# A signal for each bank of a product in a two-block transformer kernel, and gate logits inside the value product

## What is computed

```python
def hybrid_mixer(h, w_in, b_f, conv_w, conv_b, conv_ln_g, conv_ln_b, w_o):
    proj = h @ w_in
    q, k, v, f_logit, conv_val, conv_gate = jnp.split(proj, splits, axis=-1)
    log_f = jax.nn.log_sigmoid((f_logit + b_f).astype(jnp.float32))
    attn = fox_attention(q, k, v, log_f)          # causal, + cumsum(log_f)[t] - cumsum(log_f)[s]
    u = conv_val * jax.nn.sigmoid(conv_gate)
    u = causal_depthwise_conv(u, conv_w, conv_b)  # 31 taps
    u = jax.nn.silu(layer_norm_2(u, conv_ln_g, conv_ln_b))
    return jnp.concatenate([attn, u], axis=-1) @ w_o

def swiglu_ffn(h, w_ffn_in, w_ffn_out):
    g, u = jnp.split(h @ w_ffn_in, 2, axis=-1)
    return (jax.nn.silu(g) * u) @ w_ffn_out
```

## Time and profile before

| | |
|---|---|
| median of 3 runs | 2511.76 us (2510.68 to 2514.68) |
| span of the profiled execution | 2521.1 us |
| mean granted clock of TensorE | 0.963 |
| PE busy | 2317.9 us (92%), 11283 matmuls |
| DVE / ACT / POOL busy | 1435.2 (57%) / 773.5 (31%) / 1390.9 us (55%) |
| chain that ended last | PE 26%, DVE 1%, ACT 1% of the span |

### The profile page before, as it was taken

How to read it: one execution, slowest core, us unless ns; L and a number is a source line. 1 busy time by engine, 2 the same in 40 slices (tenths; PEclk the granted TensorE clock), 3 DMA queues, 4 the chain that set the end, 5 groups by cost and what they waited for, 6 DMA issues and landing times. The chain is left out here.

```text
span 2521.1 us, 32205 instructions
## 1 busy us (share of the span) xinstructions
PE 2317.9 (92%) x11283; PEld 1911.4 (76%) x11283; DVE 1435.2 (57%) x2162; ACT 773.5 (31%) x1405; POOL 1390.9 (55%) x1372
## 2 busy tenths in 40 slices
PE   6898999899999999989878988999999999999995
PEld 2687888788878777867746767777788878888874
DVE  1653646668793699964679878848612222222136
ACT  3321112123220688842333338833310000000012
POOL 2536553745984788536678843366755633333360
PEclk9899999999999899999989989999999999999997
DMA  7436335514456556342233476552322211111121
GB/s 276 147 95 194 105 101 174 185 52 150 150 190 199 160 167 168 101 176 84 67 109 90 142 181 169 164 209 88 92 80 72 96 43 49 47 46 51 51 67 67
DMA packets 180446, 305.92 MB, mean 121 GB/s; under 512 B 34940, under 2 KB 73528, under 8 KB 179008
## 3 DMA queue, kind: packets, MB, share of 16 engines
q1 hardware_dynamic: 140512, 222.75, 29.8%
q10 hardware_dynamic: 39776, 81.12, 8.7%
HBM read 247.14 MB, written 56.66 MB: 121 GB/s over the span
## 5 line engine op out<-in xcount | busy, mean ns | idle before, releaser
L1165 PE MATMUL PS<-HXH,WH 128*128 128x512 f32 (+1 forms) x1904 | 761.2, 400 | 72.3 <-DVE MOD L2206 25.5
L1046 POOL TENSOR_SCALAR WH<-RAW 128x512 fp32r<-128x512 f32 (+1 forms) x466 | 341.4, 733 | 818.5 <-PE PS L1167 671.2
L1166 PE MATMUL PS<-HXL,WH 128*128 128x512 f32 (+1 forms) x1904 | 751.7, 395 | 0.0
L1167 PE MATMUL PS<-HXH,WL 128*128 128x512 f32 (+1 forms) x1904 | 750.8, 394 | 0.0
L1049 POOL TENSOR_TENSOR WL<-RAW,WH 128x512 fp32r<-128x512 f32 (+1 forms) x466 | 630.7, 1354 | 38.9
L1165 PEld LDWEIGHTS PS<-HXH,WH 128*128 128x128 f32 (+1 forms) x1904 | 362.1, 190 | 160.5 <-DVE MOD L2206 27.6
L1167 PEld LDWEIGHTS PS<-HXH,WL 128*128 128x128 f32 (+1 forms) x1904 | 361.5, 190 | 80.1 <-issue 2.1
L1166 PEld LDWEIGHTS PS<-HXL,WH 128*128 128x128 f32 (+1 forms) x1904 | 362.6, 190 | 78.7 <-issue 3.6
L2430 DVE TENSOR_TENSOR TM<-PS,TM 128x512 f32<-128x512 f32 x44 | 28.3, 686 | 380.9 <-ACT TM L1849 380.9
L1849 ACT ACTIVATE TM<-PS 128x512 f32<-128x512 f32 x44 | 23.9, 595 | 556.6 <-PE PS L1167 556.6
L2443 DVE TENSOR_TENSOR Y<-PS,Y 128x2048 f32<-128x2048 f32 x40 | 91.7, 2292 | 123.8 <-PE PS L1167 123.7
(11 more groups left out here) (313 smaller groups left out, 4124.7 us busy)
## 6 DMA issues: line engine op xcount, KB each, us to landing
RAW<-in_ada_w SPq DMA_DIRECT2D x160, 256.0 KB, 2.7
RAW<-in_w_ffn_in SPq DMA_DIRECT2D x224, 128.0 KB, 2.1
RAW<-in_w_in_ab SPq DMA_DIRECT2D x88, 256.0 KB, 2.6
RAW<-in_w_in SPq DMA_DIRECT2D x56, 256.0 KB, 2.6
RAW<-in_w_ffn_out SPq DMA_DIRECT2D x56, 256.0 KB, 2.6
XR<-XX ACTq DMA_DIRECT2D x3, 4096.0 KB, 12.1
XX<-XR ACTq DMA_DIRECT2D x3, 4096.0 KB, 14.0
RAW<-in_w_in_c SPq DMA_DIRECT2D x40, 256.0 KB, 2.6
```

What stands on the lines that cost most here:

```text
L1046: g.tensor_scalar(WH[:, sw, 0:m], RAW[:, r, 0:m], 1.0, 0.0, ALU.mult, ALU.add).then_inc(gpsimd_done, 1)
L1165: mm(out, wh, xh, start=first, stop=False, **kw)
L1166: mm(out, wh, xl, start=False, stop=False, **kw)
L1167: return mm(out, wl, xh, start=False, stop=last, **kw)
```

## The change

Two parts.

*A signal per bank.* In a `lin` or `tok` job the last product of bank 0, 1 and 2 raises ("jobb", name, j), and that of bank 3 stands for ("jobb", name, 3) and ("job", name). In the second mixer, wo, the FFN's input product and the q and gate products of the attention layer, ACT waits ahead of each bank's eviction for that bank alone; DVE's multiplication in the FFN waits for bank 2 + j.

*The gate logits.* The eight tiles of 128x8 become one tile of 128x64, loaded by one DMA (8 columns of 32 bytes from each of 1024 rows) into one RAW slot, split by POOL into WFH and WFL, which lie outside the ring. Its slot stands ahead of the weights of cv h1. The 48 matmuls are appended to cv h1, six after each step k, and write banks 2 and 3 of the set "conv", on 8 partitions. The first tap of h1 in these banks waits until DVE has taken the logits out. The place of flog in DVE's and ACT's order stays.

```diff
@@ plan
             ev("conv", ("conv", -3), i=-3)
+            w_f = slot("split", ("b2", "f", 0), None)
         if (name, p) == ("cg", "h1"):
             ev("spill", ("spill", 2), n=2)
-            ev("flog", "flog", ws=weights("b2", "f"))
+            ev("flog", "flog")
...
+            mid=("stat", 2, "h1") if (name, p) == ("cv", "h0") else None, gates=w_f if (name, p) == ("cv", "h1") else None)
@@ SP
+                    if g == "f":
+                            sp.dma_start(dst.rearrange("p (k f) -> p k f", f=8),
+                                         a["w_in_2"][0].rearrange("(k p) n -> p k n", p=P)[:, :, c0:c0 + 8]
+                                         ).then_inc(raw_loaded[r], 16)
@@ POOL
+                if SLOTS[n][1][:2] == ("b2", "f"):
+                    g.tensor_scalar(WFH[:, :], RAW[:, r, 0:8 * KT], 1.0, 0.0, ALU.mult, ALU.add).then_inc(gpsimd_done, 1)
...
+                    g.tensor_tensor(WFL[:, :], RAW[:, r, 0:8 * KT], WFH[:, :].bitcast(F32), ALU.subtract).then_inc(gpsimd_done, 1)
@@ PE
+            def gate_logits(k, n):
+                if k == 0:
+                    pe.wait_ge(gpsimd_done, upto("w", n))
+                    for job_before in prev["conv"]:
+                        pe.wait_ge(*of("free", job_before))
+                c_ = slice(8 * k, 8 * k + 8)
+                for b, p in enumerate(("h0", "h1")):
+                    pe.wait_ge(vector_done, upto("H", "apply", 2, p, k))
+                    ins = three(bank("conv", 2 + b, p1=8), WFH[:, c_], WFL[:, c_],
+                                hs(p, k, 0), hs(p, k, 1), k == 0, k == KT - 1)
...
+                                if l and j < 3:
+                                    ins.then_inc(products_done, 1)
+                                    did(products_done, ("jobb", name, j))
...
+                        if e.get("gates") is not None:
+                            gate_logits(k, e["gates"])
@@ ACT
-                    act.wait_ge(products_done, upto("job", name))
+                    by_bank = layer in ("b2", "wo", "fi") or (layer == "c" and group[0] in "qg")
+                    if not by_bank:
+                        act.wait_ge(products_done, upto("job", name))
...
                             for j in range(4):
+                                act.wait_ge(products_done, upto("jobb", name, j))
                                 A(U[:, j, 30 + off:30 + off + w], bank(name, j, w), ACT.Copy).then_inc(scalar_done, 1)
@@ DVE
                             dve.wait_ge(scalar_done, upto("gsl", ch, part, j))
+                            dve.wait_ge(products_done, upto("jobb", name, 2 + j))
...
+                            elif x:
+                                dve.wait_ge(vector_done, upto("free", "flog"))
...
-                    src = PS[0:8, 4 * setof[name]:4 * setof[name] + 2, :].rearrange("p b n -> p (b n)")
+                    src = PS[0:8, 4 * setof["conv"] + 2:4 * setof["conv"] + 4, :].rearrange("p b n -> p (b n)")
```

More of the change, by code:

```diff
@@ L310, in plan @@
             ev("statpost", ("statpost", 2, "h1"), n=2, part="h1")
-        lin((name, p), "b2", name, p, w, last=True, midk=6, mid=("stat", 2, "h1") if (name, p) == ("cv", "h0") else None)
+        lin((name, p), "b2", name, p, w, last=True, midk=6,
+            mid=("stat", 2, "h1") if (name, p) == ("cv", "h0") else None, gates=w_f if (name, p) == ("cv", "h1") else None)
         if (name, p) == ("cv", "h0"):
@@ L441, in program @@
         XX, XC = at("XX", [KT, T], F32, XREG), at("XC", [KT, C], F32, XREG + 32768)
+        WFH, WFL = (at(f"WF{x}", [8 * KT], F32R, XREG + 32768 + 256 * i) for i, x in enumerate("HL"))
         o = [MREG + 32768]
@@ L708, in key_blocks @@
             return list(range(1 if z % 8 in (0, 7) else 0, 5))
-        splits = [n for n, x in enumerate(SLOTS) if x[0] == "split"]
+        splits = [n for n, x in enumerate(SLOTS) if x[0] == "split" and x[1][:2] != ("b2", "f")]
         WPOS = {n: i % WSLOTS for i, n in enumerate(splits)}
@@ L717, in program @@
             if e["kind"] in ("params", "tx", "ada", "adac", "stat", "lin", "tok", "kv", "chan", "spat", "dft",
-                             "dftc", "flog", "out", "small", "adasum", "cvarsum"):
+                             "dftc", "out", "small", "adasum", "cvarsum"):
                 order.append((e["name"], e))
@@ L994, in _ @@
                     sp.wait_ge(*of("rawfree", n - RSLOTS))
-                w = 8 if src[:2] == ("b2", "f") else HALF
+                w = 8 * KT if src[:2] == ("b2", "f") else HALF
                 dst = RAW[:, r, 0:w]
@@ L1017, in _ @@
                     s = [a["w_in_2"][0][rows, c0:c0 + w]]
+                    if g == "f":
+                        with nc.allow_non_contiguous_dma(reason="eight columns"):
+                            sp.dma_start(dst.rearrange("p (k f) -> p k f", f=8),
+                                         a["w_in_2"][0].rearrange("(k p) n -> p k n", p=P)[:, :, c0:c0 + 8]
+                                         ).then_inc(raw_loaded[r], 16)
+                        did(raw_loaded[r], ("raw", n), by=16)
+                        continue
                 elif l == "fi":
@@ L1207, in ada_sums @@
                 did(products_done, ("job", name))
+            def gate_logits(k, n):
[8 more added lines that the diff above has]
+                                hs(p, k, 0), hs(p, k, 1), k == 0, k == KT - 1)
+                if k == KT - 1:
+                    ins.then_inc(products_done, 1)
+                    did(products_done, ("job", "flog"))
             for e in TL:
@@ L1211, in _ @@
                 if kind in ("sum", "apply", "coef", "spill", "abload", "ysplit", "reload", "statpost", "conv",
-                            "hload", "xw", "resid", "adav", "adapost", "attc_pre", "signal", "abfetch", "csum", "cmean", "cvar", "adapool", "mask2"):
+                            "hload", "xw", "resid", "adav", "adapost", "attc_pre", "signal", "abfetch", "csum", "cmean", "cvar", "adapool", "mask2", "flog"):
                     continue
@@ L1288, in _ @@
                                 ins = three(bank(name, tb), xh[:, ts], xl[:, ts], WH[:, sw, :], WL[:, sw, :], f, l)
+                                if l and tb < n // P - 1:
+                                    ins.then_inc(products_done, 1)
+                                    did(products_done, ("jobb", name, tb))
                         else:
@@ L1302, in _ @@
                         if l:
-                            nm.append(("job", name))
+                            nm += [("job", name), ("jobb", name, 3)]
                         if nm:
@@ L1368, in _ @@
                                             WH[:, WPOS[n], w_], WL[:, WPOS[n], w_], kt + cs == 0, kt + cs == 2)
-                        ins.then_inc(products_done, 1)
-                        did(products_done, ("used", n), ("job", name))
-                elif kind == "flog":
-                    for k in range(KT):
-                        n = e["ws"][k]
-                        pe.wait_ge(gpsimd_done, upto("w", n))
-                        for b, p in enumerate(("h0", "h1")):
-                            pe.wait_ge(vector_done, upto("H", "apply", 2, p, k))
-                            ins = three(bank(name, b, p1=8), WH[:, WPOS[n], 0:8], WL[:, WPOS[n], 0:8],
-                                        hs(p, k, 0), hs(p, k, 1), k == 0, k == KT - 1)
                         ins.then_inc(products_done, 1)
```

13 lines of the change are left out of this document (11 added, 2 removed).

## The result

The changed kernel took **2487.63 us** (median of 4 runs, 2482.19 to 2490.84), against 2512.49 us for the kernel before (4 runs): a ratio of 0.990, 95% interval 0.9884 to 0.9916, 24.9 us. The forecast was 2484.9, range 2474 to 2498. In a later session, beside the experiments, the same kernel took 2485.83 us (4 runs) against 2516.93 before, a ratio of 0.9877 (0.9860 to 0.9894). So about 1.0 to 1.2% were gained. The two medians, 24.9 and 31.1 us apart, are one and the same change in two sessions: differences of a few us between kernels of different sessions mean little.

What follows compares the result with a forecast made beforehand. The prediction took TensorE (PE) as the bound, busy 2317.9 of 2521.1 us, with gains only in its waits and slow-clock stretches. Terms 12.4 + 2.0 + 2.0 + 3.8 + 4.7 + 2 = 26.9 us off 2511.8 gave 2484.9, range 2474 to 2498.

Steps and rivals of the forecast that it cites:

- q2h0's start (logits): Second mixer: with the logits inside cv h1, q2h0 starts 7.0 us earlier.
- k2h0 to v2h0: Second mixer: k2h0, k2h1 and v2h0 lose their waits for the previous eviction, 1.8 us each.
- attention layer, q: First block's attention layer: the DVE chain from q's eviction to MOD begins 2.0 us earlier, gaining 2.0.
- its gates' eviction: Attention layer: the gates' eviction on ACT, whose four stores precede the attention, gains 2.0 us.
- wo and first FFN chunks: wo and the first two FFN chunks: six waits behind evictions give 3.8 us, bounds 0 and 4.7.
- FFN's three chains: FFN: three PE waits for TM, product, AHH, AHL shrink by about 1.1, 1.5 and 2.1 us, together 4.7.
- clock: After PE's shortened waits, slow-clock spells may go: 2 us taken, bounds 0 and 3.8.
- DVE, then ACT, then POOL do the same work 1.4 + 5.25 = 6.65 us earlier: Second mixer before q2h0: U starts 1.4 us earlier, DVE's 5.25 us idle before the logits goes; the same work follows earlier.
- nearly a bound: Second mixer, q2 to v2: DVE's work keeps a job from falling below 22.3 us; at most 1.4 us, costed at nothing.
- Rival A: Evictions: ACT and DVE reach them after the job's end anyway, bank signals give little; 17 us gained, 2494.8; chance 0.17.
- Rival B: Behind cv h1: PE becomes the bound, q2h0 starts up to 20 us earlier; another 13 us, 2471.9; chance 0.08.
- Rival C: Before cv h1: the gate tile's load in 32-byte pieces lands late, POOL waits; slower, 2517 or more; chance 0.02.

Runs made afterwards that it cites:

- before_again: The kernel before, unchanged, run once more for its profile: 2515.58 us (10 runs), span 2511.6, ratio 1.0001.
- gates_b2: The changed kernel with ACT's wait per bank in the second mixer alone, whole-job waits elsewhere: 2500.23 us (6 runs), ratio 0.9949.
- gates_only: The changed kernel with ACT waiting for the whole job at every eviction, the signals still raised: 2510.01 us (12 runs), ratio 0.9981.
- flog_late: The changed kernel with DVE's and ACT's work on the logits moved behind cg h1 and its eviction: 2489.19 us (4 runs), ratio 0.9907.
- after_again: The changed kernel, unchanged, timed and profiled once more in a later session: 2485.83 us (4 runs), ratio 0.9877.

## Why the prediction was right

**The sum** was 26.9 us; the medians give 24.9 in one session and 31.1 in the other. Its terms, against both profiles of the kernel before and both of the changed one where a range stands (idle time: first profiles):

| term | forecast | measured |
|---|---|---|
| q2h0's start (logits) | 7.0 | 3.1 to 5.0 (cv h0 to q2h0) |
| k2h0 to v2h0 | 5.4 | 3.2, and 0.8 to 4.5 from q2h1 to k2h0 |
| attention layer, q | 2.0 | 0.4 to 0.7 against before_again (4.1 to 4.4 against the first profile, for the reason below) |
| its gates' eviction | 2.0 | 1.9 to 3.3, and 1.1 to 1.8 within the attention |
| wo and first FFN chunks | 3.8 | 2.9 of idle time |
| FFN's three chains | 4.7 | 3.6 of idle time |
| clock | 2 | 3.4 at the three chains alone, 2.1 of it by the signals |

The sum was forecast better than its terms, and that is in part luck. The logits' term was 2.0 to 3.9 us too large and q's 1.3 to 1.6; k2h0 and the attention's own products, where the clock has a part, and the clock behind the FFN's chains gave that back. The touched stages together are 25 us shorter against before_again and 31 against the first profile of the kernel before.

**The logits.** The mechanism was right but for one step: the matmuls cost 11.0 us in cv h1 (32.7 us for 21.7, from the first start to the last), hidden, PE's long wait moved in front of q2h0 (17.2 us; 13 to 16 were forecast), and DVE's 5.25 us of idle time went. The step that failed is "DVE, then ACT, then POOL do the same work 1.4 + 5.25 = 6.65 us earlier". DVE's work is not the same. POOL's tiles of cg h1 moved beside XX, 2.9 us more, and U moved beside POOL's tiles of cv h1, 1.9 us more. From the start of cv h0 to the logits it takes 97.5 us in both profiles of the changed kernel, and took 99.7 and 100.9 before: 2.2 to 3.4 us, where 6.65 were forecast. The prediction noted that the sixteen small splits go and that cg h1's tiles stand directly behind the sums, and costed it at nothing, since it looked for who waits for POOL and not for whom POOL slows. So 2.0 to 3.9 us of the 7.0 were lost before q2h0.

**q2 to v2.** k2h1 and v2h0 gave 3.2 us of the 3.6 forecast, v2h0 keeping a wait of 0.48 for POOL. DVE, "nearly a bound" and costed at nothing, was level with it: it came to the SPL ahead of v2h0 without idle time, and its first SPL ended at 1420.99, POOL's tile at 1421.10. The job took 22.41 us, near the 22.3 that the prediction named as the least. k2h0's 1.8 us came with a chance of the clock as large as itself.

**Rival A** (bank signals give little, 17 us in all) falls by the time, whose intervals leave at least 21 us, and by gates_b2 and gates_only: 240.7 against 246.2 us in the mixer. **Rival B** (PE as the bound, 40 us) falls by the changed kernel's own profile, in which PE still waits 17.22 us before q2h0. flog_late shows that this wait was not the bound either: moving the logits away gave q2h0 7.2 us and the end nothing; only with DVE's idle time, POOL's place beside XX and POOL's sums all changed did the mixer lose another 8 to 10 us. **Rival C** had no part: the gate tile's load landed in 2.3 us, and POOL did not wait for it. The Trainium skill's rule on transfers below 512 bytes ("DMA: Bandwidth & Descriptors", Specifications), weighed there, did not bear on this load of 32 KB: its 2.3 us are less than what a tile of 256 KB takes (2.6 to 2.7).

**The attention layer** was read from a chance. The 4.00 us of the earlier trace rows were mostly in single DVE operations of the chain that were 1.77 us long in that execution and 0.68 in before_again; the 2.0 us forecast for q were 0.4 to 0.7. It was made good by something not forecast there: with the shorter wait before the attention (1.96 us for 3.88, and 4.04 in gates_only) its first matmuls run slow for a shorter time. PE's windows at its start, gates_only, then the changed kernel:

```profile
824.30:827.30 3.00, 2.95 (x11) 0.50 0.38 145
...
822.60:825.60 3.00, 2.96 (x16) 0.83 0.39 145
```

**wo and FFN** were right in sum (10.5 with the clock; from wo to out 9.1 between gates_b2 and the changed kernel, 10.4 to 13.0 between the kernel before and it). The first of the three chains gave 0.26 us of 1.1: PE waits there for MOD, which stands behind the AHL writes on DVE. The clock gave more than the half that was taken: fo behind the three chains ran 0.8, 1.6 and 1.0 us shorter. Not all of it is the signals' work: against gates_b2, which has no signals there, it is 0.0, 1.6 and 0.5 us, and in after_again the first and the third ran another 1.6 us faster.
